# One decoder block on one core: convolution's first tap on ScalarE, SiLU four blocks at a time, decays split up, and the first filling block fetched a stage early

## The reference, cut to what matters

```python
h = rms_norm(x, norm1_gain) * (1.0 + scale1) + shift1
proj = h @ w_in          # attention q/k/v, DeltaNet q/k/v (dq, dk, dv), dz, beta, alpha, two gates
y_a = sliding_window_attention(qa, ka, va, sinks) @ w_attn_branch
qkv = silu(causal_depthwise_conv(concatenate([dq, dk, dv]), dn_conv_w))     # 4 taps, 3072 channels
beta = sigmoid(dbeta)
g = -exp(dn_a_log) * softplus(dalpha + dn_dt_bias)                          # decays, cumulated in chunks of 64
od = rms_norm(gated_delta_rule(qd, kd, vd, g, beta), dn_out_norm) * silu(dz)
y_b = od @ w_dn_branch
x = x + gate1 * ((sigmoid(gate_a) * y_a + sigmoid(gate_b) * y_b) @ w_out)
x = x + gate2 * peer(rms_norm(x, norm2_gain) * (1.0 + scale2) + shift2, ...)
```

## Time and profile before

| | us |
|---|---|
| three runs: median (lowest, highest) | 2372.32 (2365.94, 2372.43) |
| the profiled execution, its own time | 2369.7 |
| its span, first to last instruction | 2367.9 |
| projection of the 24 DeltaNet blocks with attention | 174.7 to 404.0 |
| delta rule, tiles 0, 1, 2, 3 | 404 to 497, 580, 663, 746 |

### The profile page before, as it was taken

How to read it: one execution, slowest core, us unless ns; L and a number is a source line. 1 busy time by engine, 2 the same in 40 slices (tenths; PEclk the granted TensorE clock), 3 DMA queues, 4 the chain that set the end, 5 groups by cost and what they waited for, 6 DMA issues and landing times.

```text
span 2367.9 us, 35868 instructions
## 1 busy us (share of the span) xinstructions
PE 2246.8 (95%) x14109; PEld 1952.5 (82%) x14109; DVE 1736.3 (73%) x3273; ACT 938.4 (40%) x1630; POOL 711.2 (30%) x646
## 2 busy tenths in 40 slices
PE   6898997899999999989999999899999999999998
PEld 2686776788887788879999999888888888888887
DVE  4388886544554864339999999678888788887887
ACT  2235775232223334345555555333333333333332
POOL 0354774000000000016666334433333333333320
PEclk9998998899999999999999999999999999999999
DMA  8232431111113223324443667988888888899883
GB/s 285 90 123 73 138 104 45 28 36 28 33 32 121 86 79 125 107 82 134 135 145 108 225 200 255 367 317 309 322 319 320 320 307 321 324 333 337 309 323 126
DMA packets 224999, 442.37 MB, mean 187 GB/s; under 512 B 22423, under 2 KB 138304, under 8 KB 224576
## 3 DMA queue, kind: packets, MB, share of 16 engines
q1 hardware_dynamic: 177040, 270.19, 34.0%
q0 software_dynamic: 45568, 163.60, 19.1%
q10 hardware_dynamic: 2224, 6.29, 0.7%
HBM read 394.16 MB, written 45.88 MB: 186 GB/s over the span
## 4 chain that ended last, share of the span: by engine, by line
PE 36%; DVE 19%; issue 0%; DMA 0%; ACT 0%; POOL 0%; DVEq 0%; ACTq 0%; POOLq 0%
PE bank L2049 22%; DVE hot_j L2265 6%; PE bank L2035 4%; PE bank L2033 4%; PE bank L2034 4%; DVE hot_i L2260 3%; PE bank L1917 2%; DVE eq L2233 1%; DVE eq L2229 1%; DVE pick L2235 1%; DVE ti L2202 1%; DVE ti L2195 1%; DVE sc_work L2196 1%; DVE pos L2202 1%; DVE pos L2195 1%; DVE tv L2192 1%
## 5 line engine op out<-in xcount | busy, mean ns | idle before, releaser
L1879 POOL TENSOR_TENSOR ua_lo<-ua,ua_hi 128x512 fp32r<-128x512 f32 x128 | 191.4, 1515 | 397.3 <-ACT ua L2084 397.0
L2049 PE MATMUL bank<-vt_hi,wg_hi 128*128 128x512 f32 x768 | 247.7, 403 | 5.6 <-DVE wg_lo L2319 5.3
L1872 POOL DMA_INDIRECT ug<-in_peer_u_dram,gidx x128 | 144.3, 1127 | 330.2 <-DVE ug L2275 327.1
L2049 PE MATMUL bank<-vt_lo,wg_hi 128*128 128x512 f32 x768 | 238.9, 392 | 0.0
L2049 PE MATMUL bank<-vt_hi,wg_lo 128*128 128x512 f32 x768 | 238.2, 391 | 0.0
L2301 DVE TENSOR_TENSOR vt_lo<-vt_raw,vt_hi 128x1024 fp32r<-128x1024 f32 x128 | 156.2, 1220 | 92.1 <-ACT vt_hi L2171 92.1
L1901 POOL DMA_INDIRECT vg<-in_peer_v_dram,gidx x128 | 129.8, 1014 | 239.6 <-DVE g_acc L2290 227.3
L1947 PE MATMUL bank<-h_hi,ua_hi 128*128 128x384 f32 x512 | 180.0, 351 | 0.6 <-ACT ha L2097 0.2
L2182 ACT ACTIVATE wg_hi<-wt 128x384 fp32r<-128x384 f32 x128 | 67.3, 526 | 276.2 <-DVE wt L2314 276.2
L2033 PE MATMUL bank<-h_hi,uT_hi 128*128 128x384 f32 x512 | 176.8, 345 | 0.0
L2171 ACT ACTIVATE vt_hi<-vt_raw 128x1024 fp32r<-128x1024 f32 x128 | 135.2, 1056 | 98.4 <-PE bank L2049 98.4
(11 more groups left out here) (438 smaller groups left out, 5623.6 us busy)
## 6 DMA issues: line engine op xcount, KB each, us to landing
u_raw<-in_peer_u_dram SPq DMA_DIRECT2D x128, 512.0 KB
vt_raw<-in_peer_v_dram SPq DMA_DIRECT2D x128, 512.0 KB
gates<-g_stage SPq DMA_DIRECT2D x12, 2048.0 KB, 8.8
gate<-gates SPq DMA_DIRECT2D x32, 768.0 KB, 7.1
pj_raw<-in_w_in_dram SPq DMA_DIRECT2D x16, 1024.0 KB, 5.2
ada_w<-in_w_ada_dram POOLq DMA_DIRECT2D x32, 512.0 KB, 4.5
hid_keep<-ha POOLq DMA_DIRECT2D x64, 192.0 KB, 4.3
hl<-hid_keep SPq DMA_DIRECT2D x64, 192.0 KB
```

The source lines that it names most:

```text
L1872: nc.gpsimd.indirect_dma_start(ug[s % RING][:], None, u_rows, bass.IndirectOffsetOnAxis(m.gidx[:, s:s + 1].bitcast(U32), 0)).then_inc(s_ug ...
L1879: nc.gpsimd.tensor_tensor(ua_lo[b % 2][:, 4 * q:4 * q + 4, :], ua[b % 2][:, 4 * q:4 * q + 4, :], ua_hi[b % 2][:, 4 * q:4 * q + 4, :].bitca ...
L2049: ins = pe.matmul(y_bank[t][q][:], w[n % 2][:, tok], v[n % 2][:, 512 * q:512 * q + 512], start=(first and i == 0), stop=(last and i == 2))
```

## The change

- `conv`: the first tap is now an activation on ScalarE (copy with a scale per partition) from the bank into `m.dn`; VectorE's three multiply-adds wait for it, work in `m.dn` in place and raise `st.read`. `conv_acc` is gone.
- SiLU is done in place on four blocks at once, in the slots with b mod 4 equal to 1, from 5 to 25, between scale(b-1) and exps(b).
- VectorE's order in a slot: denominator(b-1) now comes ahead of conv(b).
- The decays' chain is split: its first part after conv(0), the second after conv(1); the copy of the turned decays goes to slot 3 and the sums to slot 5. TensorE's four transposes for them go from slot 2 to slot 3.
- The first filling block is fetched by SyncE at the end of the projection's queue at offset 96 KB (where `conv_acc` was); its high part is ScalarE's first instruction of the delta phase and its low part comes ahead of tile 0's first wait. Three small constants move to other addresses.
- The fillings of a tile: 20 at the start (before: none in tile 0, then 24), 12 behind the first spread (36 in tile 0, then 12), 8 more ahead of the first products of the inverse, and 12 (before 16) behind them. `low(b0 + 1)` of tile 0 goes ahead of `vb`, and `low(b0 + 2)` of each tile behind the two `AT` products.

```diff
-    acc = [m.at(f"conv_acc{i}", [P, SEQ], 96 + 2 * i) for i in range(2)]
+    m.fl_raw0 = m.at("fl_raw0", [P, KC, P], 96)
...
             for s in range(4, N):
                 slab(s)
+            sp.dma_start(m.fl_raw0[:], w[:, :, COL_Z:COL_Z + P]).then_inc(z["fill0"], 16)
+            sp.wait_ge(z["fill0"], 16)
...
             for b in range(SLOTS + 2):
+                if b < BLOCKS:
+                    i = index(DN + b // 2, b % 2)
+                    act.wait_ge(st.ready, i + 1)
+                    nc.scalar.activation(m.dn[:, b, :], bank[i % 3][:], ACT.Copy,
+                                         scale=m.colB[:, 72 + b:73 + b]).then_inc(z["tap"], 1)
                 if b - 2 in at_score:
                     turned(at_score[b - 2])
                 if b < BLOCKS:
-                    act.wait_ge(z["conv"], b + 1)
-                    nc.scalar.activation(m.dn[:, b, :], acc[b % 2][:], ACT.Silu).then_inc(st.read, 1)
                     s = DN + b // 2
                     if b % 2 and s + 2 < N:
                         split(s + 2)
                 if b - 1 in at_score:
                     scale(at_score[b - 1])
+                if b % 4 == 1 and 4 < b < BLOCKS + 4:
+                    act.wait_ge(st.read, index(DN, 0) + b - 1)
+                    four = m.dn[:, b - 5:b - 1, :]
+                    nc.scalar.activation(four, four, ACT.Silu)
...
             def conv(b):
                 i = index(DN + b // 2, b % 2)
-                dve.wait_ge(st.ready, i + 1)
-                if b >= 2:
-                    dve.wait_ge(st.read, i - 1)
-                src, dst = bank[i % 3], acc[b % 2]
+                dve.wait_ge(z["tap"], b + 1)
+                src, dst = bank[i % 3], m.dn[:, b, :]
                 tap = lambda j: m.colB[:, 24 * j + b:24 * j + b + 1]
-                own(dve, c, v.tensor_scalar(dst[:], src[:], tap(3), None, ALU.mult))
...
-            decays()
             for b in range(SLOTS + 2):
+                if b - 1 in at_score:
+                    denominator(at_score[b - 1])
                 if b < BLOCKS:
                     conv(b)
-                if b == 2:
+                if b == 0:
+                    decays()
+                if b == 1:
+                    late_decays()
+                if b == 3:
+                    turned_decays()
+                if b == 5:
                     sums()
-                if b - 1 in at_score:
-                    denominator(at_score[b - 1])
...
+                fill(20)
                 if not first:
-                    fill(24)
                     pe.wait_ge(z["S"], t * 2)
...
-                fill(36 if first else 12)
+                fill(12)
...
+                fill(8)
                 for l in range(6):
...
                     if l < 4:
-                        fill(16 if l == 0 else 0 if last_tile else 3)
+                        fill(12 if l == 0 else 0 if last_tile else 3)
...
                 if t:
                     act.wait_ge(z["vn"], t * 2)
+                else:
+                    high(0)
...
-                if t:
-                    low(b0 + 1)
+                low(b0 + 1 if t else 0)
...
+                if t == 0:
+                    low(1)
                 dve.wait_ge(z["nat"], t + 1)
...
-                low(b0 + 2)
                 for q in range(2):
                     dve.wait_ge(z["KK"], t * 2 + (q + 1))
                     dve.wait_ge(z["Es"], t * 4 + 2 * q + 2)
                     hs = slice(G * q, G * q + G)
                     v.tensor_tensor(AT[:, hs, :], AT[:, hs, :], stacked(2 + q), ALU.mult).then_inc(z["AT"], 1)
+                low(b0 + 2)
```

More of the change, by code:

```diff
@@ L485, in phase_project @@
     off, keep4 = m.at("off", [DNH, SEQ // 16], 174), m.at("keep4", [DNH, SEQ // 16], 174.25)
-    names = ("vload vsplit conv ada_own ada_acc ada_sum sq ms krs ksqrt qrs qsqrt prep zero score soft exp den prob "
+    names = ("fill0 vload vsplit tap conv ada_own ada_acc ada_sum sq ms krs ksqrt qrs qsqrt prep zero score soft exp den prob "
              "turn turned o out sig f0 ex gT gTd gTr gc keep0 keep").split()
@@ L794, in conv @@
                     else:
-                        ins.then_inc(z["conv"], 1)
+                        ins.then_inc(st.read, 1)
             def soft(i):
@@ L845, in decays, with late_decays @@
                 own(dve, c, v.tensor_scalar(g[:], t3[:], 2.0 / 17, 2.0 / 15, ALU.mult, ALU.add))
-                for k in (13, 11, 9, 7, 5, 3, 1):
+                for k in (13, 11, 9):
+                    own(dve, c, v.tensor_tensor(g[:], g[:], t3[:], ALU.mult))
+                    own(dve, c, v.tensor_scalar(g[:], g[:], 2.0 / k, None, ALU.add))
+            def late_decays():
+                for k in (7, 5, 3, 1):
                     own(dve, c, v.tensor_tensor(g[:], g[:], t3[:], ALU.mult))
@@ L869, in amplitude, with turned_decays, sums @@
                 own(dve, c, v.tensor_scalar(na[:], na[:], -2.0, None, ALU.mult))
-            def sums():
+            def turned_decays():
                 dve.wait_ge(z["gTd"], 1)
-                dve.wait_ge(z["keep"], 2)
                 own(dve, c, v.tensor_copy(gT[:], T_BANK[0][0:DNH, :]))
                 v.engine_nop().then_inc(z["gTr"], 1)
+            def sums():
+                dve.wait_ge(z["keep"], 2)
                 own(dve, c, v.tensor_tensor_scan(run[:], keep16[:], gT[:], 0.0, ALU.mult, ALU.add))
@@ L939, in phase_delta @@
     u, wT = m.at("u", full, 80), m.at("wT", full, 84)
-    eye, near = m.at("eye", [P, CHUNK], 96), m.at("near", [P, CHUNK], 96.25)
-    step = m.at("step", [P, 6, CHUNK], 96.5)
+    eye, near = m.at("eye", [P, CHUNK], 92.75), m.at("near", [P, CHUNK], 93)
+    step = m.at("step", [P, 6, CHUNK], 93.25)
     CH = [slice(CHUNK * c, CHUNK * c + CHUNK) for c in range(2)]
@@ L945, in phase_delta @@
     sel, last2 = m.at("sel", [P, P], 92), m.at("last2", [P, 1], 92.5)
-    raw = [m.at(f"fl_raw{i}", [P, KC, P], 116 + 4 * i) for i in range(2)]
+    raw = [m.fl_raw0, m.at("fl_raw1", [P, KC, P], 120)]
     hi = [m.at(f"fl_hi{i}", [P, KC, P], (124, 192)[i], F32R) for i in range(2)]
@@ L978, in _ @@
             for f in range(FILLS + 3):
-                if f <= FILLS:
+                if 1 <= f <= FILLS:
                     load(f)
@@ L1156, in high @@
             def high(f):
-                act.wait_ge(f_loaded[f % 2], 16 * (f // 2 + 1))
+                if f:
+                    act.wait_ge(f_loaded[f % 2], 16 * ((f + 1) // 2))
                 if f >= 2:
@@ L1191, in _ @@
                 if t == 0:
-                    high(0)
                     high(1)
@@ L1271, in _ @@
                         last.then_inc(z["diff"], 1)
-                if t == 0:
-                    low(0)
-                    low(1)
                 def stacked(b):
```

2 lines of the change are left out of this document (1 added, 1 removed).

## The result

The changed kernel takes **2345.82 us** in the median (2345.09 to 2347.36, 4 runs), the kernel before 2372.38 beside it (2365.94 to 2378.09, 4 runs): ratio **0.9887, 95% interval 0.9866 to 0.9908**, 26.6 us less. The forecast was 2351 (2338 to 2364): five us too high, and one part of its sum, the delta rule, missed by twice that. The profiled execution has a span of 2343.3 us where before had 2367.9.

The account below looks back on a forecast made before the run. The loop was taken as held by hand-overs between TensorE, VectorE and ScalarE, none full. Middle 0, start 3, end 4.4 and delta rule 11.4 sum to 18.8 us, so 2369.7 - 18.8 = 2351 us, range 2338 to 2364.

Parts of the forecast that it names:

- the delta rule: All four tiles of the delta rule: 11.4 us less, ends 5 and 16.
- the middle: Projection loop, soft of slot 6 to soft of slot 22: 0 us gained, ends +12 and -5; round stays 36.2 us.
- Start: Start of the projection loop: 3 us gained, since conv(0) no longer waits behind all decays; soft of slot 6 ends earlier.
- end: End of the projection loop, behind soft of slot 22: 4.4 us gained, ends 3.5 and 5.5.
- the cover's loss is what the exps' wait costs: Loop's middle: removed tap and table loads were mostly under cover; VectorE's wait for ScalarE's exponentials costs the lost cover.
- 9.1 us of slot 1: Loop's middle, slot 1: ScalarE's summed work, including table load and SiLU of four, up to the tap slot 2 awaits.
- the rule on ScalarE's tables: ScalarE's table switches: 1283 ns a load plus 1380 for a drain, 2.66 us a switch; four rounds 5.5 us longer.
- Rival 2: Loop's middle grows: TensorE's waits drop its clock, four rounds 9 us longer, 2360 us; chance 0.17.
- Rival 1: Loop's middle falls to TensorE's floor of 32.9 us a round, or close, 2338 us; chance 0.16.
- Tile 0: First tile of the delta rule: 87.3 us against 93.0, 5.7 less, ends 2.5 and 8.
- 1.9 a tile: Delta rule, each tile: 0.9 us from fewer fillings at the head, 1.0 in the middle; ends 0.8 and 2.9.
- the second rule: Delta rule: the loop nest decides whether TensorE's clock stays up; by it alone 1.6 us more a tile.

Follow-up runs that it names:

- e9: The changed kernel run again without an edit: 2342.65 us, ratio 0.9868 to the kernel before.
- e1: The changed kernel with the whole delta rule phase of before and no early fetch, so the loop's part alone: 2361.95 us, ratio 0.9959 to the kernel before.
- e8: The changed kernel with SiLU done block by block, one slot late, instead of four blocks at once: 2336.16 us, ratio 0.9844 to the kernel before.
- e5: The changed kernel with VectorE's denominator behind the convolution again: 2347.45 us, ratio 0.9893 to the kernel before.
- e6: The changed kernel with the SiLU of four blocks one slot later, behind the tap of slot 2: 2331.08 us, ratio 0.9825 to the kernel before.
- e2: The changed kernel with the first filling block fetched late, in the delta phase: 2346.68 us, ratio 0.9885 to the kernel before.
- e4: The changed kernel with the fillings dealt as before, the low part still moved: 2350.97 us, ratio 0.9903 to the kernel before.
- e3: The changed kernel with low(b0 + 2) back ahead of the two AT products, fillings dealt anew: 2343.01 us, ratio 0.9872 to the kernel before.
- e10: On e6, in slots with b mod 4 equal to 1: tap ahead of exps, conv ahead of denominator: 2341.41 us, ratio 0.9844 to the kernel before.
- e11: The kernel before with eight unused 512-column products more per tile, ahead of TensorE's wait for AT: 2369.59 us, ratio 0.9971 to the kernel before.
- e12: The kernel before with eight unused 512-column products more among the small ones at each tile's head: 2382.27 us, ratio 1.0036 to the kernel before.

## Why the prediction was right, and where it was not

**The loop: right in size, the middle for another reason.** Start 3.0 us (3 predicted), middle 0.3 (0), end 3.9 (4.4), together 7.4 (7.4). So exact a match is partly luck: e9, the same program, has 6.1, 0.0 and 4.7, and e1 against before, with equal stages ahead, 1.9, 1.8 and 4.2. For start and end the causes are those named. `soft` of slot 22 ended at 390.7 where 385 was forecast, and the delta phase began at 402.6 where 397 was: both late by the 6 us that arose ahead of the loop. TensorE's wait ahead of slot 3's scores, 10.86 us in the earlier trace rows, is 0.70, and the next one of 3.10 stands ahead of the scores of slot 4:

```profile
205.77 1.14 PE L618 MATMUL bank<-kn,aq 64*128 64x256 f32 x8 [0.70 <-DVE sd L818]
...
216.73 2.08 PE L618 MATMUL bank<-kn,aq 64*128 64x256 f32 x8 [3.10 <-DVE sd L818]
...
395.43 1.09 PE L629 MATMUL bank<-ident,sc 128*128 128x128 f32 x8 [1.18 <-ACT sc L717]
```

The last transposes wait 1.18 us for the scaling, 4.26 in the earlier trace rows. The estimates held: tap 0.67 us (0.6), SiLU of four 1.91 (1.85), exps of up to 2.2 us of wait, eight times in the middle. The sign that eight loads stand for twenty-four was right, and e8, with the loads back off the chain, bears out that they count little. The low part's mean fell from 3.48 us to 2.28, which the sum didn't have: what VectorE lost in work, 3.7 us a round, it got back as idle time.

The step of the middle that doesn't stand is what ate the gain. The prediction says that "the cover's loss is what the exps' wait costs". With the denominator back behind conv (e5) that wait is gone and the middle is 4.1 us longer, not shorter. With the SiLU of four behind the tap (e6) the wait stays at 17.9 us and the middle is 5 to 7 us shorter. So it was the table load and the SiLU ahead of the tap of slot 2: the prediction has them in its 9.1 us of slot 1, and didn't single them out. By the rule on ScalarE's tables cited there (the Trainium skill, "ScalarE: Activation LUTs", section "What ACT_TABLE_LOAD costs") 1.38 us of drain would stand with each of the two switches of a round; the rows of slot 21 have the load end at 382.17 and the SiLU start at 382.18, and scaling ended 0.02 before the load. No drain is seen.

**Rival 2 was there in small.** The middle has a mean clock of 0.96 where it was 1.00: the clock fell at two places, for 3.4 and 6.8 us. Their cost can't be told from the scatter: the same loop takes 142.7 and 144.8 at 0.96 (e2, e9), 145.0 at 0.98 (e4) and 143.0 at 0.99 (e1, e3). It isn't the 9 us of the rival. (The waits that left the clock at 1.00 before were of up to 2.2 us, and not 2.0; in the delta rule it fell behind 1.96 and 0.89.) **Rival 1** was wrong as a forecast for this kernel, and right about the floor: e6 and e10 come to 34.4 and 33.5 us a round, towards the 32.9 of TensorE's own work.

**The delta rule: mis-sized, 22.6 us against 11.4.** Tile 0 gave 9.9 (5.7 predicted), tiles 1 to 3 gave 12.7 (5.7), outside their ends of 2.4 to 8.7. The step that failed is "1.9 a tile". It counted TensorE's waits and the number of fillings, and left the clock out of the sum: it stands in the lower bound ("the clock falls again at these two short waits") and beside the second rule, at 1.6 us a tile. Behind AT it fell no more. The waits went as forecast: in tiles 1 to 3 those for AT fall from 9.1 to 1.2 us, and a new one of about 1.0 a tile behind the 12 fillings takes 3.1. Tile 1 of after, in order of time:

```profile
515.57 0.39 PE L1040 MATMUL bank<-h_lo,fl_hi 128*128 128x512 f32 x1
515.89 0.68 PE L1112 MATMUL bank<-eye,AT 64*64 64x64 f32 x16
516.77 0.68 PE L1112 MATMUL bank<-eye,AT 64*64 64x64 f32 x16 [0.20 <-DVE AT L1320]
...
517.72 0.39 PE L1040 MATMUL bank<-h_hi,fl_hi 128*128 128x512 f32 x1
```

A stretch of length L at a mean clock of c has lost (1 - c) x L; that is the most it can have cost. Tiles 1 to 3 of before lose 3 x 3.4 us at their heads, 3 x 1.7 behind the stops at AT and 1.7 at the end of tile 3, 17 in all; after loses 3.4, 1.7 and nothing at the heads, nothing at AT and 1.7 at the end, 7. That is 10 us beside a gain of 12.7; the waits give 4.8 (9.1 to 1.2 + 3.1), and part of the one lies under the other. The 5 us at AT are shown by e11, which leaves all else and fills the wait. The 5 us at the heads are not explained, and partly luck: they came and went between profiles of one kernel (e9's tile 3 has a fall at its head, after's has none), and e12 shows only that wide products don't prevent it. In tile 0 (1 - c) x L goes from 12.1 to 5.9 us, and the early fetch has 3.5 (e2). There the prediction put 6.2 us on top of tile 1's length (3.2 for the first low part, 3.0 for fillings at half clock); measured are 2.1, 81.6 against 79.5. The first low part came as forecast: the first product starts 3.4 us into the phase.

The rule of "TensorE: Matmul & The Clock Gate" (the Trainium skill, section "Loop structure matters more than you think"), by which the order of the loops decides whether the clock stays up, was given 1.6 us a tile in the prediction, without a working, and 1.9 + 1.6 lies over the 2.9 given as the end, not within it. The measured clock term is at most 3.4 a tile, half of it at AT. The trace agrees with the rule at AT, where taking away or filling the stop kept the clock up, and not at the heads, where it falls with TensorE fully busy.

**Everything behind the delta rule** kept its length (1626.2 against 1626.8). What lies ahead of the loop didn't, and it hid 6 us of the gain in the profile that was compared. So the forecast of 2351 was close partly by luck, because two errors met: the delta rule gave 11 us more, and the unchanged stages took 6 more in this execution. How much of that is in the medians isn't known: e11 and e12, built on the kernel before, have the long stage, so executions of before may have it too, but no profile of before itself shows it.

## What to carry to other kernels

- A wait on TensorE costs its length and may cost what runs at half the clock behind it: look for the fall in the trace and price both. If the wait can't be removed, fill it with products, even unused ones, and look at the spacing of the products behind it.
- Two edits that remove the same stop don't add up; price the stop once. And where an operation is grouped or moved off an engine, look for the one instruction of the next turn that now stands behind it: moving the SiLU behind the tap took 5 to 7 us from a middle in which the whole rearrangement had gained 0.3 to 1.8.
- Cut both traces at the same events and compare the stages that nobody changed first; here they differed by 6 us, a quarter of the gain.

## What the runs showed of the hardware that was not expected

- The granted clock of TensorE falls to 0.50 at the head of the delta rule's tiles 1 to 3 while TensorE is 100% busy, and was so for the 4 us before. It does so in 39 of the 42 such tiles of the fourteen profiles, with eight products of 512 columns among the small ones too (e12). The fall lasts 6.8 us in the tiles where it starts 8.6 to 11.0 us behind the tile's cut, and 3.4 where it starts 11.1 to 12.8 us behind it.
- It falls behind a wait of 1.96 us and another of 0.89 (before, tile 1), and stays at 1.00 behind one of 0.90 alone (e11) and behind 0.83 and 1.11 (e4).
- The same untouched code took 104.3 to 104.6 or 107.7 to 108.0 us, nothing between, and its last 13 us, with TensorE fully busy, had a granted clock of 1.00 in before and 0.75 in after.
- The delta rule's tiles 1 and 2, of the same instructions, take 77.1 us at a granted clock of 1.00, 77.7 at 0.98 and 79.3 to 79.5 at 0.96 (e8, after, e6).
- VectorE's low part takes 2.28 us in the mean of the middle of after and 3.48 in before, and the small instruction of the denominator (128x4) 1.01 and 0.80: the same work got cheaper in one place and dearer in the other, with GpSimd busy 94 us of the middle instead of 104. No run isolates the cause.
